# Mixer of a decoder-layer kernel: narrow columns in column groups, the decay spreads issued together, another order of products, gates and sample updates

## What is computed

```python
h = _rms(x, norm1_w);  p = h @ w_in          # split into the parts below
qkv_a, new_conv = _short_conv(qkv_a, s_conv, conv_w)           # branch A: gated delta rule, 4 heads x 128
g = -exp(a_log) * softplus(alpha_a + dt_bias);  beta = sigmoid(beta_a)
o_a, new_gdn = _gated_delta_rule(qa, ka, va, g, beta, s_gdn)   # (I + lower) inverted per chunk
gk = (gk_lr @ gla_gk_up + gla_gk_b)                            # branch B: GLA, 4 heads x 64/128
o_b, new_gla = _gla(qb, kb, vb, log_sigmoid(gk) / 16, s_gla)
o_a, o_b = rms(o_a) * silu(z_a), rms(o_b) * silu(g_b)          # per head
merged = sigmoid(gate_a) * (o_a @ w_up_a) + sigmoid(gate_b) * (o_b @ w_up_b)
x = x + merged @ w_o
x = x + _moe(_rms(x, norm2_w), ...)          # 32 experts, top 4, clamped SwiGLU, 386 MB of weights
```

## Time and profile before

| what | value |
|---|---|
| median of 3 runs | 1357.07 us (1356.89 to 1358.92) |
| the profiled execution | 1360.63 us, of which the span from its first to its last instruction is 1357.2 us |
| TensorE busy in the span | 1283.2 us (95%) |
| DVE / ACT busy | 433.8 us (32%) / 271.2 us (20%) |
| mean granted clock of TensorE | 0.991 |
| moved by DMA | 447.76 MB |

### The profile page before, as it was taken

How to read it: one execution, slowest core, us unless ns; L and a number is a source line. 1 busy time by engine, 2 the same in 40 slices (tenths; PEclk the granted TensorE clock), 3 DMA queues, 4 the chain that set the end, 5 groups by cost and what they waited for, 6 DMA issues and landing times.

```text
span 1357.2 us, 16458 instructions
## 1 busy us (share of the span) xinstructions
PE 1283.2 (95%) x6361; PEld 653.5 (48%) x6361; DVE 433.8 (32%) x812; ACT 271.2 (20%) x503; POOL 32.2 (2%) x73
## 2 busy tenths in 40 slices
PE   7999989989999999999999999989999999999996
PEld 6777678756655434344344343424434343443433
DVE  2545565275124321232213312122221212322123
ACT  3466552130022111011110111101111010111102
POOL 5000000001000000000000000000000000000000
PEclk9989999999999999999999999999999999999999
DMA  9623200126586999999999999999999999999993
GB/s 274 182 62 99 94 32 1 62 70 210 224 347 248 422 429 427 429 428 428 428 429 428 430 427 430 427 429 428 428 429 428 429 428 429 428 430 427 430 428 158
DMA packets 61885, 447.76 MB, mean 330 GB/s; under 512 B 7637, under 2 KB 30249, under 8 KB 37276
## 3 DMA queue, kind: packets, MB, share of 16 engines
q1 hardware_dynamic: 59836, 440.34, 78.8%
q0 software_dynamic: 2016, 6.99, 1.5%
HBM read 442.30 MB, written 5.02 MB: 330 GB/s over the span
## 4 chain that ended last, share of the span: by engine, by line
PE 65%; DMA 28%; DVE 5%; ACT 1%; issue 1%; DVEq 0%; SPq 0%; ACTq 0%
PE bank L671 30%; DMA ring<-in_w_gate_up_dram 27%; PE bank L618 14%; PE bank L1078 6%; PE bank L1009 2%; PE bank L1172 1%; PE bank L874 1%; PE bank L685 1%; PE bank L886 1%; PE bank L882 1%; PE bank L1151 1%; PE bank L633 1%; DVE qkgb L1989 1%; PE bank L662 1%; PE bank L1144 0%
## 5 line engine op out<-in xcount | busy, mean ns | idle before, releaser
L671 PE MATMUL bank<-ring,zgb 128*64 128x512 f32 x2560 | 563.5, 594 | 42.5 <-DMA ring<-in_w_gate_up_dram 34.2
L671 PEld LDWEIGHTS bank<-ring,zgb 128*64 128x64 f32 x2560 | 180.1, 137 | 422.6 <-issue 339.2
L1980 DVE COPY zgb<-bank 128x512 f32<-128x512 f32 x32 | 22.1, 691 | 602.5 <-PE bank L671 602.5
L618 PE MATMUL bank<-hTb,ring 128*128 128x320 f32 x640 | 178.3, 437 | 0.8 <-DVE hTb L1575 0.8
L618 PEld LDWEIGHTS bank<-hTb,ring 128*128 128x128 f32 x640 | 121.3, 191 | 52.7 <-issue 4.6
L671 PE MATMUL bank<-ring,oABb 128*64 128x512 f32 x512 | 113.4, 595 | 0.0
L1507 ACT COPY zgb<-bank 128x512 f32<-128x512 f32 x32 | 18.7, 586 | 427.7 <-PE bank L671 427.7
L1078 PEld LDWEIGHTS bank<-oABb,h2b 128*128 128x128 f32 (+1 forms) x768 | 88.7, 196 | 13.0 <-issue 13.0
L1078 PE MATMUL bank<-oABb,h2b 128*128 128x128 f32 (+1 forms) x768 | 94.1, 284 | 0.0
L1517 ACT COPY hTb<-bank 64x512 f32<-64x512 f32 x64 | 37.1, 580 | 251.4 <-PE bank L671 250.4
L1151 PE MATMUL bank<-hTb 128*128 128x512 f32 x136 | 68.2, 606 | 0.0
(11 more groups left out here) (382 smaller groups left out, 880.0 us busy)
## 6 DMA issues: line engine op xcount, KB each, us to landing
ring<-in_w_gate_up_dram SPq DMA_DIRECT2D x128, 2048.0 KB, 30.5
ring<-in_w_down_dram SPq DMA_DIRECT2D x64, 2048.0 KB, 35.3
ring<-in_w_in_dram SPq DMA_DIRECT2D x22, 1024.0 KB, 5.5
ring<-in_w_o_dram SPq DMA_DIRECT2D x4, 1024.0 KB, 12.5
ring<-in_w_up_a_dram SPq DMA_DIRECT2D x2, 1024.0 KB, 4.9
ring<-in_w_up_b_dram SPq DMA_DIRECT2D x2, 1024.0 KB, 5.2
out_dram<-ring POOLq DMA_DIRECT2D x1, 2048.0 KB, 13.1
xbuf<-in_x_prompt_dram SPq DMA_DIRECT2D x2, 512.0 KB, 4.1
```

The costliest lines, as they stand in the source:

```text
L618: mm = pe.matmul(o[0:m, 0:TOK], w[:, k, c0:c0 + m], rhs[:, k, :], start=(k == 0), stop=(k == kk - 1))
L671: mm = pe.matmul(o[64 * f:64 * f + 64, 0:width], lhs, w[f] if isinstance(w, list) else w[:, width * f:width * f + width], start=start, sto ...
L1980: link(V.tensor_copy(pre[:, 1, :], bank[PRE[1]][:, :]), pre_done[1], n * 2 + (x + 1))
```

## The change

- **Narrow columns.** `ab` has the weights as its stationary side (32 columns, of which 8 are zeros) and all 320 tokens as the moving side, in four column groups of 32 partitions, each with two of the eight contraction chunks. ACT copies the four partial sums out (`abT`); three small matmuls by a selection matrix `sel4` (built by GpSimd at the start) add them up, tokens on partitions (`abt`), and one adds up and lays out `gk_lr` (`lr`).
- **Spreads.** The row forms of g and beta (`gbr`, `bbr`) are formed before `z3`; `gB`, `bB` of all four heads are issued together after `vb2`, and read by ACT and DVE together. DVE's `normalise` of the keys moves ahead of its last GLA level.
- **Order behind them.** The out gates `g0` to `g3` stand between other work; `gla_out` does all local products first and then all state products; all products `A` come first, `Q` after the transposes `t2`.
- **Sample updates ahead.** `ss`, `gss` of heads 0 to 3 move from the steps m = 0 to 3 to places behind `v1`, `ga3`, `gb3` and `ua1`; DVE's spreads and states with them (states of branch A's prompt, L1793, after head 0's). `rt2`, `v2` move up, `gdn_out` is grouped like `gla_out`. In every step `ub` comes before `ua`, and only `ua0` waits for branch A's gate.
- **w_o.** `wo2` begins when seven of eight merged blocks are there; the eighth is waited for inside.

The diff, cut to its core (`fill` and `o` are the rotation of the banks, which follows the order of issue):

```diff
-    fill = [["gc", "z3"], ["vb0"] + [f"tail{g}" for g in range(3)], ["vb1"], ["vb2"]]
+    fill = [["gc", "gbr", "bbr", "z3"], ["vb0"] + [f"tail{g}" for g in range(3)], ["vb1"], ["vb2"]]
...
+        o += [f"gB{h}", f"bB{h}"]
+    o += ["g0"] + [f"gT{s}" for s in range(3)] + ["ob00", "ob01", "gs0", "oi0", "oi1"] + [f"kT{s}" for s in range(3)]
+    o += ["g1", "ob10", "ob11", "gs1", "ob20", "ob21", "g2"] + [f"A{s}" for s in range(3)] + [f"om{h}" for h in range(HEADS)]
+    o += ["g3"] + [f"t2{s}" for s in range(3)] + [f"Q{s}" for s in range(3)]
...
+    o += ["gb0", "o0", "s0", "ga1", "ks1", "rt2", "gb1", "rt1", "v2", "ga2", "v1"] + upd[0] + ["gb2", "o1", "s1", "o2", "ga3"]
+    o += upd[1] + [f"on{h}" for h in range(HEADS)] + ["gb3"] + upd[2]
...
-            for s in range(3):
-                n = TILE_N[s]
-                for k in range(KD):
-                    mm = pe.matmul(o[0:n, 24 * s:24 * s + 24], hT[:, k, TILE_0[s]:TILE_0[s] + n], w_small[:, k, :],
-                                   start=(k == 0), stop=(k == KD - 1))
+            for j in range(2):
+                for g in range(4):
+                    mm = pe.matmul(o[32 * g:32 * g + 32, 0:TOK], w_small[:, 2 * g + j, :], hT[:, 2 * g + j, :], start=(j == 0),
+                                   stop=(j == 1))
             done(mm, "ab")
...
+            o = take("abt")
+            for s in range(3):
+                n, a = TILE_N[s], TILE_0[s]
+                mm = pe.matmul(o[0:n, 8 * s:8 * s + 8], abT[:, a:a + n], sel4[:, 0:8], start=True, stop=True)
...
+            done(pe.matmul(o[0:RANK, 0:TOK], sel4[:, 8:24], abT[:, :], start=True, stop=True), "lr")
...
+                        mm = pe.matmul(ob[r][:, hp, 0:n], vTM[:, s, 128 * h:128 * h + 128], ATg[:, s, h, 0:n],
+                                       start=(hp == 0), stop=(s == 0), skip_group_check=True)
...
+                for hp in range(2 if s == 1 else 0):
+                    for r in range(2):
+                        mm = pe.matmul(ob[r][:, hp, 0:n], Slp[64 * r:64 * r + 64, hp, :],
+                                       eq[64 * r:64 * r + 64, hp, a:a + n], start=False, stop=True, skip_group_check=True)
...
+            out_gate(0)
...
+            out_gate(1)
+            gla_out(1)
+            gla_out(2)
+            out_gate(2)
+            pe.wait_ge(kb_ready, HEADS)
+            products("A")
...
+            out_gate(3)
...
+            products("Q")
...
+            sample_updates(0)
             gate("gb", 2)
             gdn_out(1)
             new_state(1)
             gdn_out(2)
             gate("ga", 3)
+            sample_updates(1)
...
+            sample_updates(2)
             for m in range(KD):
...
+                for i, (nm, q, src) in enumerate((("ub", p + 1, oB), ("ua", p, oA))):
+                    if m == 0:
+                        pe.wait_ge(o_ready, i + 1)
...
-            pe.wait_ge(mrg_ready, KD)
+                if m == 1:
+                    sample_updates(3)
+            pe.wait_ge(mrg_ready, KD - 1)
...
+                if k == KD - 1:
+                    pe.wait_ge(mrg_ready, KD)
...
-            o = p3(full(act, "ab"), 3, 24)
-            step(nc.scalar.copy(lr_tm[:, 0:2, :], o[:, 0:2, 8:24]))
-            step(nc.scalar.copy(lr_tm[0:64, 2, :], o[0:64, 2, 8:24]), lr_ready)
+            o = full(act, "ab")
+            free(nc.scalar.copy(abT[:, :], o[:, 0:TOK]), "ab")
...
             spread(0)
+            spread(1)
+            sample_states(0)
+            o = p3(full(dve, "s1"), HEADS, 128)
+            step(TTo(Sp[:, :, :], Sp[:, :, :], last(glp[:, 1, :], 128), ALU.mult))
+            free(TTo(Sp[:, :, :], Sp[:, :, :], o[:, :, :], ALU.add), "s1")
+            spread(2)
+            sample_states(1)
+            spread(3)
...
+            sample_states(2)
             for m in range(KD):
-                if m < HEADS:
-                    sample_states(m)
-                    if m + 1 < HEADS:
-                        spread(m + 1)
+                if m == 2:
+                    sample_states(3)
```

More of the change, by code:

```diff
@@ L735, in _ @@
             done(mm, "gc")
+            o = take("gbr")
+            for s in range(3):
+                n, a = TILE_N[s], TILE_0[s]
+                mm = pe.matmul(o[0:HEADS, a:a + n], g_tm[0:n, s, :], (triu if s < 2 else tri8)[0:n, 0:n], start=True,
+                               stop=True)
+            done(mm, "gbr")
+            o = take("bbr")
+            for s in range(3):
+                n, a = TILE_N[s], TILE_0[s]
+                mm = pe.matmul(o[32:32 + HEADS, a:a + n], beta[0:n, s, :], ident[0:n, 0:n], start=True, stop=True)
+            done(mm, "bbr")
             z(3)
@@ L748, in _ @@
             vb(2)
[L749 to L755, removed]
             def gla_out(s):
@@ L787, in gla_out @@
                     done(mm, f"gs{s}")
[L790 to L800, removed]
             def gla_states():
@@ L960, in _, with sample_updates @@
             rhs_rows(1, LT[:, 1, :, :], 0)
-            rhs_rows(2, qkv[:, 8:12, :], PROMPT)
+            new_values(2)
             gate("ga", 2)
             new_values(1)
-            new_values(2)
+            def sample_updates(h):
+                pe.wait_ge(vm_ready, 2 * h + 1)
+                for f in range(2):
+                    o = take(f"ss{h}{f}")
+                    u = slice(32 * f, 32 * f + 32)
+                    done(pe.matmul(o[:, :], kdT[u, 2, h, :], VM[0][h % 2][u, :, :], start=True, stop=True), f"ss{h}{f}")
+                pe.wait_ge(vm_ready, 2 * h + 2)
+                r = 64 * (h % 2)
+                c = 128 * (h // 2) + r
+                for f in range(2):
+                    o = take(f"gss{h}{f}")
+                    u = slice(32 * f, 32 * f + 32)
+                    done(pe.matmul(o[r:r + 64, :], kdG[2][u, c:c + 64], VM[1][h % 2][u, :, :], start=True, stop=True),
+                         f"gss{h}{f}")
+            sample_updates(0)
             gate("gb", 2)
@@ L1346, in _ @@
             level_exp(1)
+            o = full(act, "gbr")
+            act.wait_ge(consts, 4)
+            free(nc.scalar.copy(gb_rows[0:HEADS], o[0:HEADS, 0:TOK]), "gbr")
+            o = full(act, "bbr")
+            free(nc.scalar.copy(gb_rows[32:32 + HEADS], o[32:32 + HEADS, 0:TOK]), "bbr")
             freed(act, "gc")
@@ L1359, in _ @@
             take_vb(2)
-            for s in range(3):
-                n = TILE_N[s]
-                o = full(act, f"gT{s}")
-                free(nc.scalar.copy(kdG[s][0:n, :], o[0:n, 0:256]), f"gT{s}")
-            o = full(act, "gbr")
-            act.wait_ge(consts, 4)
-            free(nc.scalar.copy(gb_rows[0:HEADS], o[0:HEADS, 0:TOK]), "gbr")
-            o = full(act, "bbr")
-            free(nc.scalar.copy(gb_rows[32:32 + HEADS], o[32:32 + HEADS, 0:TOK]), "bbr")
-            oB_r = oB.rearrange("p (a r) t -> p r a t", r=2)
             for h in range(HEADS):
@@ L1704, in _ @@
             differences([(0, PROMPT, 128, 127), (PROMPT, TOK - PROMPT, 8, 7)], False)
+            for t in range(4, 8):
+                normalise(t)
             attention(3)
@@ L1767, in _ @@
                 level(s, 1, lt_ready)
+            for s in range(3):
+                n = TILE_N[s]
+                o = p3(full(dve, f"Q{s}"), HEADS, 128)
+                free(TTo(attnT[0:n, s, :, 0:n], o[0:n, :, 0:n], attnT[0:n, s, :, 0:n], ALU.mult), f"Q{s}")
             for i, b in enumerate(LEVELS):
```

196 lines of the change are left out of this document (87 added, 109 removed).

## The result

The changed kernel takes 1345.04 us (1344.53 to 1345.24); the kernel before, run beside it, 1357.97. The ratio is 0.9907, 95% interval 0.9896 to 0.9919: 12.9 us faster, where 22 were forecast, and 1 us outside the range. Its profiled execution took 1344.53, with a span of 1342.8.

What follows compares the result with a forecast made beforehand. From 706 us the weight stream bounds the kernel, its start set by TensorE, so TensorE's time from 70 to 372 us counts. 4.1 + 8.5 + 8.4 + 1.2 = 22.2 us off the median 1357.07 gives 1335.0; range 1330 to 1344.

Steps and rivals of the forecast that it cites:

- on the other queues: Sample updates: SyncE loads the fifth `ub` panel 4.5 us later at most, 9 us of gates ahead of its reader.
- part 4: Sample updates, TensorE 231.16 to 319.24: work moved into DVE's idle time, waits and lower clock go, 8.4 us gained.
- part 1: Narrow columns: 16 instructions in column groups replace 48, `qb0` begins at 76.5 instead of 80.7, 4.1 us gained.
- Part 2: Spreads and products, TensorE 144.74 to 197.33: idle time 5.5, clock 1.5, GLA product 1.5, together 8.5 us gained.
- Part 5: At w_o: `wo2` waits 1.38 us for DVE's last merge; 1.2 us gained.
- the text's estimate from the drain: Chain ahead of branch A's gate: drains at two table switches bring `o_ready` to about 294.7, sum 20.3 instead of 22.2.
- one part falls short: Rival, chance 0.30: one part of the change gains less than forecast, 1337 to 1344 us.
- the clock: Rival case, 0.13: clock falls at the new wait or among short products before X; 1.5 to 2.2 us each.
- the new wait: Narrow columns: `abt` waits for ACT's copy, which stands behind the last SiLU, from 73.7 until 75.3; without it another 1.6 gained.
- DVE as the bound: Rival case, 0.08: DVE still sets the pace in the sample updates, gain 3.5 instead of 8.4, 1340 us.
- the slow stretch: Rival, 0.04: clock falls from 144.74 to the products without dense gates between; 32.9 us more, 1367.9.
- an unmoved stream: Rival, 0.03: the weight stream starts no earlier because its first pieces are themselves late; no gain, 1357 us.

Runs made afterwards that it cites:

- the spreads' run with GpSimd held: Kernel before with only spreads together, new order of products and gates, GLA's grouped product, and GpSimd waiting for `ga6`: 1349.96 us, 0.9951.
- the spreads' run: Kernel before with only spreads together, new order of products and gates and GLA's grouped product, GpSimd not held: 1355.88 us, 0.9983.

## Why the prediction was wrong

- **The step that failed** is the paragraph "on the other queues" of part 4: "SyncE loads the fifth `ub` panel behind `ua3` instead of `ub3`, 4.5 us of products later at most, with 9 us of gates ahead of its reader ... GpSimd's stores hang on states that come earlier". Panel and stores were looked at one by one and costed at nothing. The panel was given the landing that it had when nothing else moved, 5.2 us, against a cover of 8.6; with 5 MB of GpSimd's transfers ahead of it, moved there by the same change, it took 16.5. The price was 8.0 us of waiting and 2.3 of lower clock, 10.3 together; the measured time stands 10.0 above the forecast, and the run that moves only GpSimd's transfers out of the way lands at 1334.54 against a forecast of 1335.0. That it meets the forecast so closely is partly luck: part 1 gave 1.9 us less than forecast, and the other rows of the table, with w_o's from that run, 2.0 more.
- *Part 1* was mis-sized: 2.2 us instead of 4.1. `ab` (1.28), the norms (2.42) and the wait (1.61) came as forecast, and `qb0` begins 6.61 us behind `ab` where it was 10.55. The clock fell behind that wait and cost 1.7 us on the projections (10.57 against 8.88), which the text priced at 2 as a bound and left out of the sum. The runs with `qb0` ahead, 3.5 us shorter in this stretch, show that wait and clock were all of it.
- *Part 2* held in its sum, 8.8 against 8.5, with other shares: idle time gave 4.4 where 5.5 was forecast, shorter busy time 4.4 where 3.0 was. Idle time left was 1.8 us in all, where 0.8 had been kept back. 1.3 of it is the bank of `ob01`, at the place that was named: it waits for the reader of `bB2` on DVE (L1758), not within the 0.5 us that the text had counted. X runs at 2.66.
- *Part 4* held on TensorE and DVE, 9.7 against 8.4, more than the 9.3 that the text took for the most: no wait at `ss`, `gss` or `ua0`. Branch A's gate was done before TensorE wanted it, at 278.24 by DVE's row, but only by some 0.3 us where the text had counted 1; that margin was luck. *Part 5* held: w_o follows with no wait.
- *The table loads*: the chain in front of branch A's gate ran as the rows of before said (load 1.28, the next row at once, and the load itself 0.02 us behind the row ahead of it, which ends at 271.94), not with a drain of 1.38 for each as the Trainium skill, "ScalarE: Activation LUTs", section "What ACT_TABLE_LOAD costs", counts; by the rows after:

```profile
271.96 1.28 ACT L1285 ACT_TABLE_LOAD   x1
273.25 1.97 ACT L1285 ACTIVATE ring<-ring 128x320 f32<-128x320 f32 x4
```

- *A sum* is off by a tenth: 1357.07 less 22.2 is 1334.9, not 1335.0. So is the text's estimate from the drain that the Trainium skill counts: 292 and twice 1.38 are 294.8, which is 1.8 behind `ua0` at 293, not 1.9. Nothing rests on either.
- *The rivals*: of "one part falls short" the clock was the one that came, at the new wait; DVE as the bound, the slow stretch and an unmoved stream did not. The one that decided, two queues' transfers in each other's way, was not among them.

What stays open: why the clock fell at `g0` with `qb0` ahead (141 to 144.5 us there) and in the spreads' run with GpSimd held, and not in the other profiles with the same order of instructions; and why the times of the spreads' run lie up to 11 us apart.

## What to carry to other kernels

When work is moved earlier, everything that hangs on its end moves too, the stores on other queues as well: write down for each transfer behind the moved work when it will now be issued, and against which load that somebody waits for. A load that lands in 5 us alone can take three times that beside others; its row from a quiet moment is no price for a busy one, and here the profile of before had a row of the busy case (14.1 us) beside the quiet one. A margin of 1 us between two queues is luck: the spreads alone turned it round. Give the order a semaphore.

## What the runs showed of the hardware

A 1 MB panel issued behind some 5 MB on another queue landed in 16.5 us after and in 16.6 in the run of the spreads alone; it took 5.2 where it came first and 5.1 where the others were held back. The DMA view shows where the time went. Behind the request, from 296.05 to 300.50, SyncE's queue moved nothing while GpSimd's moved 1.12 MB; from there to the landing at 312.58 both moved (queue: packets, MB, share of the 16 engines; q0 is GpSimd's, q1 SyncE's; the first line is the first stretch):

```profile
q0 software_dynamic: 273, 1.12, 101.6%
...
q0 software_dynamic: 711, 2.46, 64.3%
q1 hardware_dynamic: 662, 1.19, 34.2%
```

They sent about as many packets, but GpSimd's were twice as large (3.5 KB on average against 1.8), so the panel got a third of the bytes. The share of 1.01 at only 260 GB/s, where the weight stream has 1.01 at 428, shows that the engines were full, not fast; why, no run shows:

```profile
296.00:300.00 4.00, 4.00 (x17) 2.81 (x16) 1.14 (x3) 0.00 (x0) 1.23 (x2) 1.00 1.01 260
```

TensorE had run the norms at full clock, stood idle for 1.6 us before `abt`, ran the short products of `abt` and `lr`, and was granted the lower level (0.50, 1.2 GHz) in the middle of the projections behind them:

```profile
76.00:78.00 2.00, 2.00 (x5) 1.34 (x4) 0.00 (x0) 1.97 (x3) 0.00 (x0) 0.50 0.00 0
```

With `qb0` in the gap the same stretch kept 1.00, with the same short products behind it.
